# Seven quarter products in place of eight for the first layer's queries and the latent layer's gates

## The reference

```python
h_l = rmsnorm(x_lat, g_pre) * (1.0 + sc_l) + sh_l        # h_c likewise, from the context

def window_gqa_mixer(h_lat, h_ctx, ...):                 # layers 0 and 3
    q_l, k_l, v_l, z_l = split(h_lat @ w_in)             # q: 1024 columns, k and v: 256 each, z: 1024
    q_c, k_c, v_c, z_c = split(h_ctx @ w_in)
    q_l, k_l = apply_rope(q_l, cos, sin), apply_rope(k_l, cos, sin)
    ...                                                  # banded attention with scale 64 ** -0.5
    y_l = (o_l * silu(z_l)) @ w_out

def mla_mixer(h_lat, h_ctx, ...):                        # layer 1
    q_a_l, kv_a_l, kpe_l, z_l = split(h_lat @ w_in)      # 256, 128, 64 and 1024 columns
    ...
    y_l = (o_l * silu(z_l)) @ w_out
```

## Time and profile before

| what | value |
|---|---|
| median of three runs | 1707.37 us |
| the profiled execution's own time | 1708.81 us |
| its span | 1707.0 us |
| TensorE busy | 1662.7 us, 97% of the span |
| VectorE, ScalarE, GpSimd busy | 561.6, 413.9, 332.1 us |
| mean granted clock of TensorE | 0.999 |

### The profile page before, as it was taken

One profiled execution on the slowest core, in us unless ns is written; L12 is line 12 of the kernel. 1 busy time (PEld: TensorE's weight loads), 2 busy tenths in 40 slices (PEclk: granted clock), 3 DMA queues, 4 the chain that ended last, 5 costly groups with the idle time before them and its releaser, 6 DMA issues.

```text
span 1707.0 us, 18350 instructions
## 1 busy us (share of the span) xinstructions
PE 1662.7 (97%) x7031; PEld 968.6 (57%) x7031; DVE 561.6 (33%) x1605; ACT 413.9 (24%) x1070; POOL 332.1 (19%) x386
## 2 busy tenths in 40 slices
PE   5999999999999999999999999999999999999999
PEld 2454555454446545887464577644444544688854
DVE  2123433321334233664383424420332223222200
ACT  2003444220224221101152304520243331100000
POOL 0113554110100012431062224610213210000000
PEclk9999999999999999999999999999999999999999
DMA  9321312230350032212261432149443123344441
GB/s 396 157 114 50 148 42 107 99 139 25 111 209 38 25 143 106 85 64 99 104 242 35 190 129 100 50 117 247 157 152 148 50 99 134 130 160 161 155 148 50
DMA packets 19078, 209.75 MB, mean 123 GB/s; under 512 B 2856, under 2 KB 3384, under 8 KB 6576
## 3 DMA queue, kind: packets, MB, share of 16 engines
q1 hardware_dynamic: 15568, 195.74, 30.1%
q0 software_dynamic: 3424, 12.84, 3.3%
HBM read 201.08 MB, written 4.21 MB: 120 GB/s over the span
## 4 chain that ended last, share of the span: by engine, by line
PE 93%; DVE 2%; DMA 2%; POOL 1%; ACT 1%; issue 1%; SPq 0%; DVEq 0%; ACTq 0%
PE bank L676 39%; PE bank L1412 9%; PE bank L1154 7%; PE bank L771 5%; PE bank L785 5%; PE bank L1434 4%; PE bank L928 3%; PE bank L721 2%; PE bank L1066 2%; PE bank L1042 2%; DMA ring<-stream 2%; PE bank L1052 2%; PE bank L758 2%; PE bank L689 1%; PE bank L947 1%; PE bank L732 1%
## 5 line engine op out<-in xcount | busy, mean ns | idle before, releaser
L676 PE MATMUL bank<-ring,arena 128*128 128x512 f32 (+2 forms) x1296 | 531.6, 568 | 3.9 <-DVE arena L2027 1.3
L676 PEld LDWEIGHTS bank<-ring,arena 128*128 128x128 f32 x1296 | 243.1, 190 | 269.9 <-issue 254.6
L2660 POOL TENSOR_SCALAR arena<-arena,stat 128x512 f32<-128x512 f32 (+1 forms) x96 | 128.2, 1349 | 135.0 <-DVE stat L1596 135.0
L1412 PE MATMUL bank<-arena,ring 128*128 128x256 f32 (+1 forms) x768 | 152.8, 362 | 0.0
L676 PE MATMUL bank<-arena,ring 128*128 128x512 f32 (+2 forms) x400 | 146.8, 526 | 0.8 <-DVE arena L1474 0.8
L1412 PEld LDWEIGHTS bank<-arena,ring 128*128 128x128 f32 x768 | 136.0, 190 | 16.9 <-issue 0.5
L676 PEld LDWEIGHTS bank<-arena,ring 128*128 128x128 f32 (+1 forms) x400 | 73.8, 186 | 70.3 <-issue 65.8
L785 PE MATMUL bank<-ring,arena 128*128 128x512 f32 x192 | 90.8, 610 | 1.8 <-ACT arena L2385 1.2
L771 PE MATMUL bank<-arena,ring 128*128 128x512 f32 (+1 forms) x256 | 91.4, 499 | 0.0
L2297 ACT ACTIVATE arena<-arena,stat 128x513 f32<-128x513 f32 (+1 forms) x96 | 61.9, 646 | 80.8 <-DVE stat L1588 80.8
L771 PEld LDWEIGHTS bank<-arena,ring 128*128 128x128 f32 x256 | 46.0, 189 | 45.0 <-issue 41.7
(11 more groups left out here) (320 smaller groups left out, 1949.4 us busy)
## 6 DMA issues: line engine op xcount, KB each, us to landing
ring<-stream SPq DMA_DIRECT2D x88, 2048.0 KB, 7.9
ring<-stream SPq DMA_DIRECT2D x4, 1024.0 KB, 5.1
arena<-arena POOLq DMA_DIRECT2D x50, 64.0 KB, 1.8
rev_scratch<-arena POOLq DMA_DIRECT2D x1, 3072.0 KB, 36.7
masks_sb<-masks POOLq DMA_DIRECT2D x2, 1024.0 KB, 5.0
arena<-g_scratch POOLq DMA_DIRECT2D x1, 2048.0 KB, 9.4
arena<-rev_scratch POOLq DMA_DIRECT2D x1, 2048.0 KB, 16.2
ring<-stream SPq DMA_DIRECT2D x1, 1536.0 KB, 6.7
```

Of the source, the lines that this page charges most:

```text
L676: last = mm(dst, a, b, start=(k == 0), stop=(k == len(pairs) - 1))
L1412: last = mm(ps[:, SEQ * part + cols.start:SEQ * part + cols.stop], w[:, a:a + P], hT2[:, k, cols], start=(k == 0), stop=(k == DC - 1))
L2660: nc.gpsimd.tensor_scalar(row, row, stat[:, 3, s:s + 1], None, ALU.mult).then_inc(w_norm, 1)
```

## The change

Two blocks in layer 0 (q0, q1) and two in layer 1 (z0, z1) go through `seven_products`. Its parts are written once for all layers: `add_tokens` and `combine` for VectorE, `save_first_part` for ScalarE, `weight_differences` and `last_difference` for GpSimd. `combine` takes a function that places other work between its sums. In layer 0 that work is the rotations and the read-outs of the modulation; in layer 1 it is the gate (tanh on ScalarE into `z_opened`, product on VectorE). The order of the blocks in the ring stays. The scale 1/8 moves into `combine`, whose sums are now `scalar_tensor_tensor` in the third layer too.

```diff
-QUADS = ("qk0", "qk1", "v1", "o0", "o1")
+QUADS = {0: ("q0", "q1"), 1: ("z0", "z1"), 2: ("qk0", "qk1", "v1", "o0", "o1")}
+FIRST_QUAD = {0: 0, 1: 2, 2: 4}
+QUAD_SCALE = {0: 0.125, 1: 1.0, 2: 1.0}
...
+            for c in range(8):
+                if layer == 0:
+                    swaps += [(parts_v, 6 * (FIRST_QUAD[0] + c // 4) + (6 if c % 4 > 1 else 1), qT[:, c, 0:SEQ])]
+                else:
+                    swaps += [(saved_a, saved_counts(group_of_qkv(layer, "q", c) + 1)[1], qT[:, c, 0:SEQ])]
...
-
-                w = weights(f"{layer} {QUADS[b]}").rearrange("p (k n) -> p k n", k=DC)
-                t1, t2, t4 = weight_sums[b]
...
+            def seven_products(layer, b, between=None):
+
+                at, g = FIRST_QUAD[layer] + b, STAGES[f"{layer} quads"][b]
+                w = weights(f"{layer} {QUADS[layer][b]}").rearrange("p (k n) -> p k n", k=DC)
+                t1, t2, t4 = weight_sums[layer][b]
...
                     return last
 
-                if b:
-                    pe.wait_ge(parts_v, 6 * b - 1)
+                if at:
+                    pe.wait_ge(parts_v, 6 * at - 1)
                 product(0, part_of(hT, 0, 0), part_of(w, 0, 0)).then_inc(parts_made, 1)
                 product(1, part_of(hT, 0, 1), part_of(w, 0, 1)).then_inc(parts_made, 1)
-                if b:
-                    pe.wait_ge(parts_v, 6 * b)
-                else:
-                    pe.wait_ge(flag("token_sums_ready"), 1)
-                pe.wait_ge(sums_made, 4 * b + 2)
+                if between:
+                    between()
+                if at:
+                    pe.wait_ge(parts_v, 6 * at)
+                if not b:
+                    pe.wait_ge(flag("token_sums_ready"), layer + 1)
+                pe.wait_ge(sums_made, 4 * at + 2)
                 product(2, s2, t2).then_inc(parts_made, 1)
                 if b:
                     pe.wait_ge(saved_v, V_UPTO[STAGES[f"{layer} quads"][b - 1] + 1])
                 product(3, s1, t1).then_inc(parts_made, 1)
-                pe.wait_ge(parts_a, b + 1)
-                pe.wait_ge(sums_made, 4 * b + 3)
+                pe.wait_ge(parts_a, at + 1)
+                pe.wait_ge(sums_made, 4 * at + 3)
                 product(4, s3, part_of(w, 1, 0)).then_inc(parts_made, 1)
-                pe.wait_ge(parts_v, 6 * b + 1)
+                pe.wait_ge(parts_v, 6 * at + 1)
                 product(5, s4, part_of(w, 1, 1)).then_inc(parts_made, 1)
-                pe.wait_ge(parts_v, 6 * b + 2)
-                pe.wait_ge(sums_made, 4 * b + 4)
+                pe.wait_ge(parts_v, 6 * at + 2)
+                pe.wait_ge(sums_made, 4 * at + 4)
+                begin(g)
                 product(6, part_of(hT, 1, 1), t4).then_inc(made, 1)
+                weights_done()
...
+                        seven_products(0, 0)
+                        modulation_products(0, 4, range(DC))
+                        seven_products(0, 1, lambda: modulation_turn(0, 4))
+                        modulation_products(0, 5, range(DC))
...
+                    for b in range(2):
+                        seven_products(layer, b)
                     gate_groups(layer)
...
+            def combine(layer, b, between):
+
+                at, g, scale = FIRST_QUAD[layer] + b, STAGES[f"{layer} quads"][b], QUAD_SCALE[layer]
+                first, total, other = pair_of(first_part), pair_of(part_sum), pair_of(other_sum)
+                target = lambda i, n: quad_target(layer, b, i, n)
+
+                def add(dst, i, term, have):
+                    dve.wait_ge(parts_v, 6 * at + have)
+                    return vec_op.scalar_tensor_tensor(dst, pair_of(part_bank(layer, b, i)[:, :]), scale, term, ALU.mult, ALU.add)
+
+                dve.wait_ge(parts_made, 6 * at + 2)
+                dve.wait_ge(parts_a, at + 1)
+                add(target(0, 0), 1, first, 0).then_inc(parts_v, 1)
+                between("first")
+                dve.wait_ge(parts_made, 6 * at + 3)
+                add(total, 2, first, 0).then_inc(parts_v, 1)
+                between("second")
+                dve.wait_ge(parts_made, 6 * at + 4)
+                add(other, 3, total, 2).then_inc(parts_v, 1)
+                between("third")
+                dve.wait_ge(parts_made, 6 * at + 5)
+                add(total, 4, total, 3).then_inc(parts_v, 1)
+                add(target(1, 1), 3, total, 4).then_inc(parts_v, 1)
+                between("fourth")
+                dve.wait_ge(parts_made, 6 * at + 6)
+                add(target(0, 1), 5, other, 3).then_inc(parts_v, 1)
+                between("fifth")
+                dve.wait_ge(made, g + 1)
+                add(target(1, 0), 6, total, 4).then_inc(saved_v, 1)
+                between("last")
...
-                        for a, b, i in ((0, 3, 8), (3, 4, 9), (4, 7, 10), (7, 8, 11)):
-                            rotate(a, b)
-                            save_modulation(0, i)
+                        add_tokens(0)
+                        combine(0, 0, lambda place: rotate(0, 2) if place == "fourth" else None)
+                        save_modulation(0, 8)
+
+                        def between(place):
+                            if place == "first":
+                                save_modulation(0, 9)
+                            elif place == "second":
+                                rotate(2, 4)
+                            elif place == "fourth":
+                                rotate(4, 6)
+
+                        combine(0, 1, between)
+                        save_modulation(0, 10)
+                        rotate(6, 8)
+                        save_modulation(0, 11)
...
+                    add_tokens(layer)
...
+                        dst = quad_target(layer, b, *((0, 0), (1, 1), (0, 1), (1, 0))[i])
+                        dve.wait_ge(flag("z_tanh"), z_before[layer] + k + 1)
+                        dve.wait_ge(parts_v, 6 * (FIRST_QUAD[layer] + b) + min(6, (1, 5, 6, 7)[i]))
+                        if i == 3:
+                            dve.wait_ge(saved_v, V_UPTO[STAGES[f"{layer} quads"][b] + 1])
+                        vec_op.scalar_tensor_tensor(dst, pair_of(z_opened[k % 2]), 1.0, dst, ALU.add, ALU.mult)\
...
+                        def between(place):
+                            if place == "third":
+                                open_gate(b, 0)
+                            elif place == "fifth":
+                                open_gate(b, 1)
+                            elif place == "last":
+                                open_gate(b, 2)
+                                open_gate(b, 3)
+
+                        combine(layer, b, between)
+                        if b == 0:
+                            gate_diagonals(layer)
                     gate_groups(layer)
...
+                    for b in range(2):
+                        at = FIRST_QUAD[layer] + b
+                        save_first_part(layer, b)
+                        for i, (half, n) in enumerate(((0, 0), (1, 1), (0, 1), (1, 0))):
+                            k = 4 * b + i
+                            sc.wait_ge(parts_v, 6 * at + min(6, (1, 5, 6, 7)[i]))
+                            if i == 3:
+                                wait_saved(sc, f"{layer} quads", b + 1)
+                            if k >= 2:
+                                sc.wait_ge(flag("z_gated"), k - 1)
+                            act_op(pair_of(z_opened[k % 2]), quad_target(layer, b, half, n), ACT.Tanh, scale=0.5).then_inc(flag("z_tanh"), 1)
...
+            def weight_differences(layer, b):
+
+                at, block = FIRST_QUAD[layer] + b, BLOCK_AT[f"{layer} {QUADS[layer][b]}"]
+                w = ring[:, block % RING, :].rearrange("p (k n) -> p k n", k=DC)
+                t1, t2, t4 = weight_sums[layer][b]
+                pool.wait_ge(weights_in[block % RING], 16 * (block // RING + 1))
+                if b:
+                    pool.wait_ge(parts_made, 6 * at - 2)
+                nc.gpsimd.tensor_tensor(t1, part_of(w, 1, 0), part_of(w, 0, 0), ALU.subtract).then_inc(sums_made, 1)
+                pool.wait_ge(sums_made, 4 * at + 1)
+                nc.gpsimd.tensor_tensor(t2, part_of(w, 1, 1), t1, ALU.subtract).then_inc(sums_made, 1)
+                nc.gpsimd.tensor_tensor(part_of(w, 1, 0), part_of(w, 1, 1), part_of(w, 1, 0), ALU.subtract).then_inc(sums_made, 1)
...
+            def last_difference(layer, b):
+
+                at, block = FIRST_QUAD[layer] + b, BLOCK_AT[f"{layer} {QUADS[layer][b]}"]
+                w = ring[:, block % RING, :].rearrange("p (k n) -> p k n", k=DC)
+                t1, t2, t4 = weight_sums[layer][b]
+                if b:
+                    pool.wait_ge(made, STAGES[f"{layer} quads"][b - 1] + 1)
+                pool.wait_ge(sums_made, 4 * at + 2)
+                nc.gpsimd.tensor_tensor(t4, part_of(w, 0, 1), t2, ALU.subtract).then_inc(sums_made, 1)
...
-                    swap_pairs(layer)
+                    if layer == 0:
```

(30 more changed lines are left out.)

185 lines of the change are left out of this document (71 added, 114 removed).

## The result

The kernel after took 1704.51 us (median of 16 runs, 1701.82 to 1706.27). Beside it the kernel before took 1708.71 us (16 runs, 1706.15 to 1710.79). The ratio is 0.9977, 95% interval 0.9969 to 0.9984: faster by 4.2 us, where 8.4 us were forecast. The time is above the range. Of the miss of 5.5 us, 1.3 us is the base: the forecast started from a median of 1707.37 us. The rest is half of the gain.

A forecast was written before the change was run, and what follows sets the result against it. TensorE, busy 1662.7 of 1707.0 us, was taken as the bound. First layer -3.0, second layer -6.6, gates +0.3 and clock +0.9 gave -8.4 us: from 1707.37 to 1699.0 us, 8-in-10 range 1694.0 to 1703.0.

The forecast's parts named there:

- the step on the clock: Behind the first layer's 4 us wait: TensorE's clock may fall, priced at +0.9 us, with 0 and 1.7 as ends.
- the start of the first layer: First query block: sums and differences run in turns, ready at 50.2 us; TensorE waits 4.0 us, costing 3.6 us against before.
- The price of a block: Seven products take 24.18 us against 27.47 us for a plain block, saving 3.29 us each.
- The gates: End of the second layer's z blocks: 6.0 us to the next weights product instead of 5.75, +0.3 us.
- The covers: Later differences, rotations and sums finish before TensorE needs them, with 13, 10 and 6 us to spare.
- The turns: VectorE's token sums and GpSimd's differences in SBUF hold each other and run serially, 1.23 and 2.35 us each.
- Not held: Rival: the first layer's token sums are not held, or far less; 1693.3 us, chance 0.12.
- Slower by the clock: Rival: the clock falls in the wait at 46 us and stays down; 1717.3 us, chance 0.06 including other causes.
- The covers fail: Rival: late transfers delay VectorE's rotations and the sums behind them, giving back most gain; 1704 to 1710 us, chance 0.08.

The follow-up runs named there:

- busy_wait: The changed kernel plus eight unused products on TensorE between the first block's second and third product; 1701.30 us, ratio 0.9960 to the kernel before.
- after_again: The changed kernel, unaltered, measured and profiled a second time; 1703.42 us against 1710.16 us for the kernel before, ratio 0.9964.
- l0_only: The changed kernel with only layer 0's q0 and q1 through seven products, layer 1 as before; 1709.54 us, ratio 1.0006 to the kernel before.
- l1_only: The changed kernel with only layer 1's z0 and z1 through seven products, layer 0 as before; 1702.65 us against 1708.65 us for the kernel before.
- sums_first: The changed kernel with GpSimd's third and fourth difference of q0 waiting for the four token sums; 1696.62 us, ratio 0.9932 to the kernel before.
- fill: The changed kernel with modulation block 4's products moved between the first block's second and third product, read-out behind its first sum; 1698.75 us, ratio 0.9941 to before.

## Why the prediction was wrong

**What failed is the step on the clock.** The sum took 0.9 us, half way between 0 and 1.7, as if the fall were a chance. It came in all three profiles that have the wait. Where the wait was 3.34 us it cost 1.7 us by products 2 and 3 (8.86 - 7.17), the whole of the upper end; where it was 5.49 us it lasted 6.8 us and cost 3.05 us (10.22 - 7.17), beyond that end. busy_wait shows the cause: beside after_again, 3.0 us come back by the first key product although the work behind the wait starts at nearly the same time.

**The second mis-sized term is the start of the first layer.** By the profile after it looks nearly as written: sums ready at 50.12 us (50.2 forecast), products 0 and 1 from 39.69 (39.3), wait 3.34 us (4.0), two sums held. Part of this is luck. The work ahead of `hT` ended 1.0 us later than in the earlier trace rows, and the scales' instruction took 0.89 us, not 1.7; the two nearly cancel. With the clock's 1.7 us taken off, the first key product would stand at 96.7 us, as written. But the other start, q0 1.3 us later, was not priced: a third sum is held and the wait is 5.49 us, 1.0 us beyond the forecast at product 2 (51.17 against 50.2). The text noted that q0 "may land earlier or later" and used it for the gain only; it can be a loss. Of the seven profiles with the first layer's blocks two had it, after_again and busy_wait; how often each start comes isn't known.

Put together, the first key product comes at -3.0 + 1.7 = -1.3 us in the first kind of execution and at -3.0 + 1.0 + 3.0 = +1.0 us in the second. Both are seen (98.36 and 100.72 us against 99.67). The forecast had -3.0 + 0.9 = -2.1 us for this layer, l0_only measured +0.9 us (its interval is -0.5 to +2.6 us). These two steps alone do not carry all of that: l0_only's own profile was of the first kind, 1.6 us ahead, and lost 2.3 us at the fall near 184 us.

The pair of profiles says the same. It differs by 5.2 us in the span, 3.2 us short of the forecast's 8.4. Of these, 0.8 us is the clock behind the wait (1.7 for 0.9), 1.1 us went at the fall near 184 us and 1.3 us near 853 us. The forecast had no term for falls elsewhere. Whether they belong to the change is open.

**What held.**
- The price of a block: 24.17 us in both layers, 48.34 us for the two z blocks (48.4 forecast).
- The gates: 6.10 us (6.0), so +0.35 us in place of +0.3, and l1_only's -6.0 us for -6.3. The two gates behind the last sum are two instructions of 0.7 us as taken; the copies behind them stand in VectorE's row, 2.48 us for four, without a gap.
- The covers: TensorE waits inside no later block, and third-layer blocks kept their time (24.17 us, 24.18 before).
- The turns. VectorE and GpSimd did run one after the other here when each read and wrote SBUF only; where they alternate, a pair took 3.3 to 3.4 us, less than the 3.58 us that the two durations add up to. The Trainium skill's "SBUF — State Buffer" (section "Who interferes with whom"), cited for this, agrees with the trace also for the small instruction: 0.89 us for 0.17.
- The warning of the Trainium skill's "TensorE: Matmul & The Clock Gate" (section "HAM oscillation — how this bites in real kernels"), that work behind a wait starts slow, agrees with all three profiles that have the wait; it was given too little weight. The fall came between 0.6 us before the wait's end and 1.1 us behind it.

**The rivals.** "Not held" (1693.3 us) is what sums_first builds: 1696.62 us beside a before of 1708.65, where 14.1 us were forecast for it, 12.0 came (0.51 us of wait was left). "Slower by the clock" had the right mechanism and the wrong size: it asked for 9.3 us of work or more done at half the clock, and 1.7 and 3.0 us were seen. "The covers fail" did not happen, though its time did (1704.51 us): no product waits inside a later block.

**What stays open.** The first layer's blocks gained 6.9 us by the earlier sums; the profiles account for 2.8 us of wait and 1.7 of clock against after, or for 5.0 and 3.0 against after_again, less 0.6 for products 0 and 1 that began sooner there. The median lies between, falls further on are in it too, and which share of the executions is of each kind wasn't counted. Whether the wait at 46 us makes the falls near 184 us more frequent, which the low mean clocks of the first-layer kernels and three profiles of five allow, wasn't tried. The two measurements of the whole change, -4.2 and -6.7 us, differ by more than the sizes argued here need; their intervals overlap only from 0.9969 to 0.9976.

## What to carry to other kernels

Price a new wait of TensorE at its length plus a fall of the clock behind it: here 3.3 us of wait cost 1.7 us more, and 5.5 us of wait 3.0 us more, until work was put into the gap. Best is work that is needed anyway: the modulation block moved into the wait gave 4.7 us (fill against after_again on the same chip) for no new instruction. Where two engines work in SBUF on what one product needs, order them by need: the differences for products 4 to 6 had no business ahead of the sums for product 2, and one wait on GpSimd turned a first layer that cost 0.9 us into one that saved 6.0. And where a start depends on a transfer, work out the late landing as well as the one in the profile.

## What the runs showed of the hardware

- A VectorE instruction of 128x16 elements that reads and writes SBUF took 0.89 us in after and 1.08 us in l0_only while a GpSimd operation ran, and 0.17 us when it came 0.2 us ahead of one. VectorE's eight writes of `hT`, which read PSUM, took 3.71 us under two GpSimd operations, as without any (3.70 us in the earlier trace rows).
- The hold goes both ways: GpSimd's 2.35 us became 3.33 us behind a sum that was running.
- The granted clock fell about 1 us after work had begun again in after (51.23 us, where the wait ended at 50.17), and 0.6 us before the wait's end in after_again (50.54 us, end at 51.17). It stayed low for 3.4 us in after and 6.8 us in after_again. It did not fall behind the 1.86 us wait of busy_wait, nor around the 1.19 and 2.92 us waits of fill with 1.9 us of work between them.
- The fall near 184 us cost about a third of its length, 1.1 us for 3.4 us and 2.3 us for 6.8 us, where the one behind the first layer's wait cost half. In before, at the full clock, TensorE is busy for 2.40 and 3.33 us of the two 4 us stretches from 180 us on.
- The same kernel, run again, has falls in other places: before had one near 1268 us in its first profile, and in its second two, near 184 and 860 us, and none near 1268, at spans of 1707.0 and 1707.9 us. Two profiles can't be compared stage by stage without the clock of both.
